# Two transformer blocks on one core: where VectorE scales the attentions' probabilities

## The reference, cut to what matters

```python
# sparse: 8 heads of 64; only the 64 keys that an index picked are valid
s = einsum('bqhd,bqkhd->bhqk', q, k_sel) * dh ** -0.5
p = softmax(where(valid, s, -inf))
y_b = einsum('bhqk,bqkhd->bqhd', p, v_sel)
# differential: 4 heads, two score maps each
s = where(causal, einsum('bqhcd,bshcd->bhcqs', q, k) * d ** -0.5, -inf)
p = softmax(s)
a = p[:, :, 0] - lam * p[:, :, 1]
y_c = einsum('bhqs,bshv->bqhv', a, v)
```

## Time and profile before

| | us |
|---|---|
| three runs | 1839.53, 1842.12, 1842.03 (median 1842.03) |
| the profiled execution | 1840.88 |
| its span | 1839.2 |

### The profile page before, as it was taken

How to read it: one execution, slowest core, us unless ns; L and a number is a source line. 1 busy time by engine, 2 the same in 40 slices (tenths; PEclk the granted TensorE clock), 3 DMA queues, 4 the chain that set the end, 5 groups by cost and what they waited for, 6 DMA issues and landing times.

```text
span 1839.2 us, 36333 instructions
## 1 busy us (share of the span) xinstructions
PE 1781.1 (97%) x14784; PEld 1734.7 (94%) x14784; DVE 1360.9 (74%) x2385; ACT 1072.6 (58%) x1808; POOL 190.8 (10%) x200
## 2 busy tenths in 40 slices
PE   8999999999999999999999999999999998999998
PEld 8999999999999989999999888999999988899998
DVE  6998789867899779876768867655557687676553
ACT  5455656654454657654775675544458757755442
POOL 1012410001002410001201003000002100030000
PEclk9999999999999999999999999999999999999999
DMA  8545536564645536664646634555555564355553
GB/s 284 178 151 186 191 122 202 194 206 134 204 161 184 184 127 206 195 205 140 192 147 170 202 103 141 177 198 194 194 156 180 160 195 132 106 169 194 196 194 104
DMA packets 90342, 320.08 MB, mean 174 GB/s; under 512 B 10528, under 2 KB 12992, under 8 KB 90048
## 3 DMA queue, kind: packets, MB, share of 16 engines
q1 hardware_dynamic: 90176, 317.75, 52.5%
HBM read 310.60 MB, written 1.08 MB: 169 GB/s over the span
## 4 chain that ended last, share of the span: by engine, by line
PE 73%; DVE 15%; ACT 6%; issue 4%; POOL 1%; DMA 1%; SPq 0%; DVEq 0%; ACTq 0%; POOLq 0%
PE big L588 67%; PE small L588 4%; DVE POOL L1467 4%; DVE L L1110 4%; ACT H L1886 2%; PE small L587 1%; DVE POOL L1299 1%; DVE POOL L1665 1%; ACT POOL L2270 1%; POOL POOL L2482 1%; ACT POOL L2308 1%; ACT L1982 0%; DVE gates L1354 0%; POOL POOL L2461 0%; DVE FL L1277 0%
## 5 line engine op out<-in xcount | busy, mean ns | idle before, releaser
L588 PE MATMUL big<-HH,H 128*128 128x256 f32 x3344 | 941.5, 282 | 9.6 <-DVE gates L1354 4.8
L588 PE MATMUL big<-HL,H 128*128 128x256 f32 x3344 | 927.4, 277 | 3.9 <-DVE HL L1245 3.8
L588 PE MATMUL big<-HH,L 128*128 128x256 f32 x3344 | 926.2, 277 | 0.0
L1110 DVE TENSOR_TENSOR L<-F,H 128x1024 fp32r<-128x1024 f32 x574 | 703.7, 1234 | 205.6 <-ACT H L1886 204.3
L1886 ACT ACTIVATE H<-F 128x1024 fp32r<-128x1024 f32 x582 | 610.7, 1055 | 205.7 <-PE big L588 202.2
L588 PEld LDWEIGHTS big<-HH,H 128*128 128x128 f32 x3344 | 630.1, 188 | 14.6 <-issue 5.9
L588 PEld LDWEIGHTS big<-HL,H 128*128 128x128 f32 x3344 | 630.3, 188 | 7.8 <-DVE HL L1245 5.9
L588 PEld LDWEIGHTS big<-HH,L 128*128 128x128 f32 x3344 | 629.9, 188 | 0.0
L588 PE MATMUL big<-FH,H 128*128 128x256 f32 x848 | 238.5, 281 | 0.0
L588 PE MATMUL big<-FH,L 128*128 128x256 f32 x848 | 234.4, 276 | 0.0
L588 PE MATMUL big<-FL,H 128*128 128x256 f32 x848 | 234.3, 276 | 0.0
(11 more groups left out here) (237 smaller groups left out, 1795.4 us busy)
## 6 DMA issues: line engine op xcount, KB each, us to landing
F<-in_stream SPq DMA_DIRECT2D x582, 512.0 KB, 4.1
POOL<-POOL SPq DMA_DIRECT2D x32, 128.0 KB, 4.0
POOL<-head_rows SPq DMA_DIRECT2D x8, 256.0 KB, 5.2
X<-in_x SPq DMA_DIRECT2D x2, 512.0 KB, 4.4
POOL<-POOL SPq DMA_DIRECT2D x16, 64.0 KB, 3.1
out_x<-X SPq DMA_DIRECT2D x1, 1024.0 KB, 3.9
POOL<-in_decay SPq DMA_DIRECT2D x1, 768.0 KB, 11.6
POOL<-POOL SPq DMA_DIRECT2D x8, 96.0 KB, 5.2
```

The costliest lines, as they stand in the source:

```text
L588: return pe.e.matmul(out_, lhsT, rhs, start=start, stop=stop)
L1110: v.tensor_tensor(L[:, j % NR, :], F[:, j % NF, :], H[:, j % NR, :].bitcast(F32), ALU.subtract).then_inc(s_lo, 1)
```

## The change

VectorE's tasks of the attentions yield "behind" after the negative factor of the maxima. `Steps` keeps such tasks in a list `open`, and a new method `rest` steps each of them once more, in the order of the tasks. VectorE's loop calls `rest` at the end of every turn, after the low parts. So the scaling (from the reciprocal to L1696 or L1762) is put there. One more `yield` follows the scaling, so that the steps after it keep their turns. `step` and `finish` call `rest` first; no other task yields "behind", and the other engines' programs stay as they are.

```diff
     def __init__(self):
-        self.tasks = []
+        self.tasks, self.open = [], []
...
     def step(self):
+        self.rest()
         said = [(n, t, next(t, "over")) for n, t in self.tasks]
         said = [(n, t, next(t, "over") if word == "later" else word) for n, t, word in said]
         self.tasks = [(n, t) for n, t, word in said if word != "over"]
+        self.open = [t for n, t, word in said if word == "behind"]
+
+    def rest(self):
+        for t in self.open:
+            next(t)
+        self.open = []

     def finish(self, name):
+        self.rest()
...
# sparse and diff of VectorE, after the factor of the maxima
-                    yield
+                    yield "behind"
                     dve.wait_ge(sp_a[t].sem, sp_a[t].at(l, u))
                     v.reciprocal(sm, sm).then_inc(sp_v[t].sem, sp_v[t].up(l, u, "rc"))
...
                         sp_v[t].sem, sp_v[t].up(l, u, "p"))
+                    yield
                     yield
                     yield
                     low_sparse(l, t, u)
...
                 for j in rest:
                     if not full_banks(n):
                         low_parts(j + AHEAD)
+                beside.rest()
```

## The result

| | before | after |
|---|---|---|
| median, us (6 runs each, same chip) | 1842.07 (1839.53 to 1844.37) | 1852.53 (1849.59 to 1855.26) |
| ratio after / before | | 1.0059 [1.0046, 1.0072] |
| profiled execution, us (span) | 1840.88 (1839.2) | 1850.61 (1848.9) |

The change makes the kernel slower by 10.5 us, 0.6%. The forecast was 1853.

What follows compares the result with a forecast made beforehand. TensorE, busy 97% of the span, bounds the kernel, so only its stands count. First pass 5.5, second 4.1 and clock 1.5 make 11 us, added to the median of 1842.03: 1853 us, range 1847 to 1859.

Steps and rivals of the forecast that it cites:

- 1051.75: First pass: a sparse and a diff scaling go ahead of `low_sparse` 0; TensorE loses 1.3 us, net 0.8 later.
- 1072.39: Two scalings go ahead of `low_sparse` 0: + 1.0 us in the first pass, - 0.4 in the second.
- 1080.9: A diff scaling goes ahead of `low_sparse` 1, just as TensorE comes to its scores: + 0.87 us.
- the 0 at 1036.5: Sparse1's scaling ahead of `low_sparse` 0 delays scores up to 0.6 us, absorbed by TensorE's stand at 1045.11: sum 0.
- the + 0.6 at 1097.8: `low_sparse` 1 comes after the diff scaling's wait for exponentials, so VectorE's next turn and the transposes at 1105.03 come 0.6 us later.
- The dear turn: At 1059.84 `low_sparse` 1 queues behind a diff scaling awaiting exponentials: TensorE's scores 3.76 us later, idle some 4.4 us.
- the point I could not read: Whether ScalarE's chain at 1059 moves with TensorE's 1.3 us delay: between 0 and + 1.3 a pass, taken as 0.
- The gain: At 1090.3 two scalings precede a `low_sparse` 0 whose bank nobody awaits; transposes at 1091.79 come 0.7 us earlier.
- The clock: Granted clock falls after the long stand: 1.5 us added for the second pass, between bounds of 0 and 1.7.
- that the probabilities decide: Rival: bank waits are covered, so only the earlier probabilities for the transposes count; faster, 1840 us; chance 4%.
- that all is absorbed: Rival: each delay ends in a wait that was there anyway; no change, 1843 to 1845 us; chance 7%.
- that the stand spreads: Rival: the stand at 1059.84 holds VectorE, ScalarE and TensorE in a ring, clock falls twice; 1859 to 1862 us; chance 13%.

Runs made afterwards that it cites:

- the third experiment: The kernel after, but the first diff1 unit's scaling in each pass stays in the next turn: 1850.89 us, ratio 1.0060 to the kernel before.

## Why the prediction was right, and where it was not

- **The order in VectorE's turn** (1051.75, 1072.39, 1080.9): right, each to 0.1 us, by the table of shifts; so are the 0 at 1036.5 (the scores there stand 1.11 us for L1719, and the transposes behind them start where they did, 1043.74 + 1.37 = 1045.11) and the + 0.6 at 1097.8. The run without the sigmoid confirms that this order is the larger part.
- **The dear turn** (1059.84): right in place and size, 3.77 for 3.76, with a stand of 4.33 for 4.4. The exponentials did not move with TensorE: the diff scaling came at 1063.70 + 1.37 = 1065.07, before at 1065.05. This was the point I could not read.
- **The gain** at 1091.79: right (- 0.63 for - 0.7), and again in the run with that unit alone.
- **The clock**: the total was right and the reading behind it was not. I wrote that before's fall in the first pass, 1.7 us, was "already in the time of before". It was not: the score at 1073.02 starts 48.88 us into the first pass, behind a fall, and 48.89 into the second, without one. The fall was hidden, for with TensorE late the stand there was 0.27 instead of 1.69. After the change nothing hides it, and it costs 1.6 in each pass. The sum still came out as a difference, because the item at 1072.39 (+ 1.0 in the first pass, - 0.4 in the second) already held this lost cover under another name: with the stand filled it is - 0.7 in both. Read properly, each pass loses about 4.0 by order and waits and 1.6 by the clock. The 1.5 for the second pass was a choice between bounds of 0 and 1.7, made on one fall and one that did not come; that it was near 1.6 is in part luck.
- **The price of leaving the dear turn out**: wrong in the third experiment, 5.3 for 2.4, and the step that failed is again the clock. The turns came as forecast, as the kernel with the stand filled shows (2.44). I had written that without the long stand the clock would no longer fall in the second pass, and perhaps not in the first. But the waits that this stand had covered came back as one of 3.29 us at the next score, with a fall twice as long, 2.8 us. The miss with the sparse units alone is of the same kind: a stand of 2.46 us where I had 1.0, and a fall behind it.
- **The rivals**: that the probabilities decide fell by the ten waits for the bank; that all is absorbed fell by the passes; that the stand spreads fell for the whole change. The differential units alone come near its 1859 to 1862 (1857), by the order as forecast for that run.

The head of the program varies with how often the clock fell in it, some 3.4 us at the lower level each time: with no fall the first pass began at 1020.58 and 1020.99 us, with one at 1021.95, with two at 1022.77 to 1025.57, with three and four at 1027.37 and 1027.39. That goes together and was not tested; why it falls in one execution and not in another stays open. Why the clock fell after a stand of 1.4 us in before's first pass, and not in its second, stays open too.

## What to carry to other kernels

Before moving work ahead in an in-order queue, ask what stands behind it there and who waits for that: an operation that frees a bank goes ahead of one that only makes data earlier, and a wait at the end of a turn holds up the whole next turn. Move such work unit by unit, not as a rule: the same edit gained in one turn of a pass and lost in five. And look for the long operation ahead of the chain on the engine nobody watches; moving one sigmoid by five steps gave 0.4% with the same output. Where a step shortens a stand or moves it, ask also whether the clock will fall behind the stand that is left.

## What the runs showed of the hardware

- **A stand can cost more in clock than in time.** After a stand of 4.33 us TensorE's granted clock was 0.70 over the next 5.6 us, and between its two levels (1.2 and 2.4 GHz) that is some 3.4 us at the lower. After one of 3.29 us, the clock was 0.57 over the 8 us that begin within the stand, some 6.9 us at the lower (0.43 x 8 / 0.5); the second pass has 0.72 over its 12 us as well. A longer stand did not mean a longer fall. Matmuls of no use put into the stand kept the clock at 1.00 and gave back 1.6 and 2.8 us. The Trainium skill, TensorE: Matmul & The Clock Gate, in "HAM oscillation", says that gaps send TensorE back to half clock; the traces agree for the stands from 2.44 us up that TensorE had in the attentions. For stands of 1.42 to 1.44 they show it once in the two passes of the kernel before, in both with only the last unit of sparse1 moved, and in neither with only the sparse units moved; behind the two of 2.13 with the earlier scalings the clock stayed at 1.00.
- **A fall may be free.** Behind before's fall TensorE's next wait was for VectorE, and the fall cost nothing there (the score starts at 48.88 us of the pass with it, 48.89 without). In the kernel after, the next stand was 1.25 us with the fall and without it, and the fall cost its whole 1.6.
- **Equal instructions vary.** The stretch ahead of the first pass, the same in all these programs, moved the pass's start over 6.8 us between executions, while the two passes of an execution differed in length by 0.31 or less in all kernels but one (0.78, with only the differential units moved). An effect of 1 us in a span of 1840 can be measured, by such a length and not by the time.
